# The expert stage of a streaming encoder layer, rebuilt in 33 blocks of 64 rows

## The chip, the cores and the metric

The kernel runs on one core of one Trainium2 chip. The metric is the device time of one execution in microseconds (us), lower is better. Engines: PE (TensorE, with its weight loads as PEld), DVE (VectorE), ACT (ScalarE), POOL (GpSimd) and SP (SyncE, which here only issues DMAs).

## The reference, cut to what matters

One layer of an encoder over 576 frames of width 1024: projections, a gated convolution, a gated delta rule, and then a mixture of experts with a residual and a final norm. The change is in the mixture, whose arithmetic is:

```python
for wg, wu, wd, c in experts:                # 32 experts, 1024 -> 256 -> 1024
    hdn = jax.nn.silu(t @ wg) * (t @ wu)
    acc = acc + c[:, None] * (hdn @ wd)      # c is zero but for 2 experts a frame
```

Each frame goes to two experts, so 1152 rows are spread over 32 experts. With the reference's inputs the fullest expert gets 75 rows, the next 61.

## The kernel before, in words

Phases 1 and 2 compute the mixers (up to about 937 us), phase 3 the norm, the router and the places of the rows, phase 4 the experts, phase 5 the weighted sum and the final norm.

At the end of phase 3 POOL scatters every row twice into the DRAM tensor `scr_rows`, sorted by expert (L1777). Phase 4 then takes one block of `BR = 80` rows for each expert. Were an expert fuller than 80 rows, the loop in `further_blocks` (L1364) would run more blocks; here none is needed.

Matrices are fp32, multiplied as sums of products of float32r numbers. ACT copies a tensor into a rounded high part (`ehi`, `xbh`, `hth`), DVE subtracts that from the tensor and writes the low part (`elo`, `xbl`, `htl`), and PE adds three products: high by high, low by high, high by low. A block goes through these steps:

- SP loads gate, up and down weights, 1 MB each, into `eraw` (L1615, L1619), and the rows into `xb` (L1676); two buffers of each.
- ACT splits the 4096 gate and up columns in one go (L1398) and the 2048 down columns in another (L1403); DVE follows with L1408.
- PE turns the rows with 8 transposes (`rows_turned`, L1318) into `wideA`; ACT and DVE split them (L1416, L1420).
- `gate_up` (L1321): 24 matmuls of 512 columns, whose stationary operand is 80 columns wide; gate in the left half of `proj[k]`, up in the right half, rows on the partitions.
- ACT takes the silu of gate (L1426), DVE multiplies by up (L1479), PE turns the result with 2 transposes (L1340), ACT and DVE split it (L1430, L1484).
- `down` (L1343): 12 matmuls into `wideB`; ACT copies that to `yout` (L1438), SP stores it to `scr_y` (L1680).

The order is written out by hand in `expert_tensor` (L1355), `expert_scalar` (L1440) and `expert_vector` (L1487). On PE a block's order is: 12 matmuls of `gate_up(b)`, `down(b-1)`, the other 12, the transposes of the rows of b+1, the transposes of the hidden layer of b. The next block's `gate_up` waits for `e_xl`, the low part of its rows, which were turned just before. Semaphores are counted up by each step; SP loads block b+2's weights once `e_low` says that block b's are split. SP's queue holds all loads and stores of the stage in one order.

After the last block POOL gathers each frame's two results with 10 indirect DMAs (L1791), and phase 5 adds and normalises.

Of the kernel before, what the change touches and what calls it, by code (L numbers as in the profile page):

```python
# [18 lines left out]
F32 = mybir.dt.float32  # L19
# [21 lines left out]
BR = 80  # L41
OVER = (SLOTS - 2) // BR
BLOCKS = EXPERTS + OVER
ROWS = SLOTS + BR

# [22 lines left out]
C_MISC = C_LEVEL + P * (LEVELS + 1)  # L68
# [23 lines left out]
def encoder_layer(nc, A, O):  # L92
# [6 lines left out]
    with top:  # L99
# [17 lines left out]
        before = const[:, C_BEFORE:C_BEFORE + P]  # L117

# [87 lines left out]
        EW = 24 * DE  # L206
        AT_P3 = EW

# [14 lines left out]

        p3 = area(AT_P3)
        g2row = sb(p3, "g2row", [P, D])
        wr = sb(p3, "wr", [P, KC, GROUPS + EXPERTS])
        tn = sb(p3, "tn", [P, UNITS, D])
        tT = [sb(p3, f"tT{k}", [P, D]) for k in range(2)]
        sqs = sb(p3, "sqs", [P, D])
        lg = sb(p3, "lg", [P, UNITS, GROUPS + EXPERTS])  # L230
# [8 lines left out]
        brow = sb(p3, "brow", [P, 3, OVER])  # L239

        eraw, ehi, elo = [None, None], [None, None], [None, None]
        ehi[0] = sb(p3, "ehi0", [P, EW], F32R)
        xb = [sb(p3, f"xb{k}", [P, D]) for k in range(2)]
        xbh = [sb(p3, f"xbh{k}", [P, KC, BR], F32R) for k in range(2)]
        xbl = [sb(p3, f"xbl{k}", [P, KC, BR], F32R) for k in range(2)]
        yout = [sb(p3, f"yout{k}", [P, D]) for k in range(2)]
        p3.close()
        p4 = area(0)
        eraw[0] = sb(p4, "eraw0", [P, EW])
        ehi[1] = sb(p4, "ehi1", [P, EW], F32R)  # L250
        elo[1] = sb(p4, "elo1", [P, EW], F32R)
        p4.close()
        p4 = area(AT_ML)
        elo[0] = sb(p4, "elo0", [P, EW], F32R)
        eraw[1] = sb(p4, "eraw1", [P, EW])
        hgate = [sb(p4, f"hgate{k}", [P, DE]) for k in range(2)]
        hid = [sb(p4, f"hid{k}", [P, DE]) for k in range(2)]
        hth = [sb(p4, f"hth{k}", [P, 2, BR], F32R) for k in range(2)]
        htl = [sb(p4, f"htl{k}", [P, 2, BR], F32R) for k in range(2)]
        p4.close()  # L260

        p5 = area(EW)
        fy = [[sb(p5, f"fy{j}_{c}", [P, D]) for c in range(UNITS)] for j in range(2)]
        fsq = sb(p5, "fsq", [P, D])
        p5.close()
        p5 = area(AT_ML + EW)
# [7 lines left out]
        x_in = [sem(f"x_in{c}") for c in range(UNITS)]  # L274
# [465 lines left out]
        def tails_pool(pool, i, which):  # L740
# [17 lines left out]
        p2_w, g_in = [sem("p2_w0"), sem("p2_w1")], [sem("gate_in0"), sem("gate_in1")]  # L758
# [8 lines left out]
        e_w, e_wd = [sem("e_w0"), sem("e_w1")], [sem("e_wd0"), sem("e_wd1")]  # L767
        e_x = [sem("e_x0"), sem("e_x1")]
        e_high, e_low, e_xt, e_xh, e_xl, e_gu, e_silu, e_hid, e_ht, e_hh, e_hl, e_dn, e_y = (
            sem("e_" + k) for k in "high low xt xh xl gu silu hid ht hh hl dn y".split())  # L770
# [3 lines left out]
        f_y = [sem(f"f_y{c}") for c in range(UNITS)]  # L774
# [242 lines left out]
        def out_split_high(act, q, k):  # L1017
            if isinstance(q, int):
                act.wait_ge(p2_w[k], 16 * (q // 2 + 1))
            else:  # L1020
                act.wait_ge(p2_w[k], 8 * (q - k) + 16)
# [114 lines left out]
        def phase3_scalar(act):  # L1136
# [15 lines left out]
            for part in range(2):  # L1152
                weights_high(act, 0, 0, part)
# [32 lines left out]
        def phase3_vector(dve):  # L1186
# [84 lines left out]
            link(dve.tensor_copy(table[0:1, TB_COUNT:TB_COUNT + 1], ex[0:1, 3, E - 1:E]))  # L1271
# [37 lines left out]
        DOWN_AT = 12  # L1309
        GU = 16 * DE  # L1310

        def rows_turned(pe, b, k, arrived=None):

            pe.wait_ge(*(arrived or (e_x[k], 8 * (b - k) + 16)))
            wait(pe, e_xl, b)
            v = xb[k][0:BR, :].rearrange("s (p c) -> s c p", c=KC)
            for c in range(KC):
                mm = pe.transpose(wideA[:, c * P:c * P + BR], v[:, c, :], ident[0:BR, 0:BR])  # L1318
            mm.then_inc(e_xt, 1)

        def gate_up(pe, b, k, between=None):  # L1321
            pe.wait_ge(e_low, 2 * b + 1)
            pe.wait_ge(e_xl, b + 1)
            wait(pe, e_hid, b - 1)
            for j in range(3 * KC):
                c, term = divmod(j, 3)
                if between and j == DOWN_AT:
                    between()
                x = (xbh, xbl, xbh)[term][k][:, c, :]
                w = (ehi, ehi, elo)[term][k][:, 0:GU].rearrange("p (w c n) -> p w c n", w=2, c=KC)[:, :, c, :]  # L1330
                mm = pe.matmul(proj[k][0:BR, :].rearrange("p (w n) -> p w n", w=2), x, w, start=(j == 0),  # L1331
                               stop=(j == 3 * KC - 1))
            mm.then_inc(e_gu, 1)

        def hidden_turned(pe, b, k):
            pe.wait_ge(e_hid, b + 1)
            wait(pe, e_hl, b)
            v = hid[k][0:BR, :].rearrange("s (p c) -> s c p", c=2)
            for c in range(2):
                mm = pe.transpose(proj[2][:, c * BR:(c + 1) * BR], v[:, c, :], ident[0:BR, 0:BR])  # L1340
            mm.then_inc(e_ht, 1)

        def down(pe, b, k):  # L1343
            pe.wait_ge(e_hl, b + 1)
            pe.wait_ge(e_low, 2 * b + 2)
            wait(pe, e_y, b)
            for n in range(2):
# [662 lines left out]
```

## Time and profile before

| | |
|---|---|
| runs of the kernel | 1411.27, 1421.46, 1423.44 us; median 1421.46 |
| the profiled execution | 1412.39 us |
| its span | 1410.7 us, so 1.7 us lie around it |
| granted PE clock over the span (1.00 is 2.4 GHz, 0.50 is 1.2 GHz) | 0.947 |
| busy share of the span | PE 88%, DVE 56%, ACT 44%, POOL 4% |
| first transpose of the expert stage | 989.85 us |
| last copy to `yout` begins | 1374.88 us |

A line of a timeline reads: start, duration (both us), engine, line, operation, output <- input with partitions x elements, and count; in brackets the idle time before it and what ended that. Matmuls overlap each other, so the time between two starts (the pitch) counts and not the duration.

### The profile page before, as it was taken

How to read it: one execution, taken by the hardware profiler on the slowest of the kernel's cores; microseconds unless marked ns; L12 is line 12 of the kernel's file. 1: busy time of each engine (PE TensorE's matmuls, PEld its weight loads, DVE VectorE, ACT ScalarE, POOL GpSimd, SP SyncE). 2: the span in 40 equal slices, each digit the busy share in tenths (PEclk: the TensorE clock that was granted, in tenths of full speed). 3: DMA queues.
4: the chain of work that ended last, by engine and by line, in shares of the span. 5: the costliest groups of instructions: out<-in, count | busy, mean ns of one | idle time of the engine just before them, and what ended most of it. 6: DMA issues, size and time to landing. Idle time of an engine off the chain costs nothing.

```text
span 1410.7 us, 22131 instructions
## 1 busy us (share of the span) xinstructions
PE 1247.0 (88%) x8469; PEld 1112.5 (79%) x8469; DVE 784.5 (56%) x930; ACT 622.3 (44%) x851; POOL 57.4 (4%) x124
## 2 busy tenths in 40 slices
PE   4989999999999999999989989980888888888870
PEld 4989999999999999999989989980555555555550
DVE  4437365473654736547465445236667667767735
ACT  4434343343433534335342322251566666666632
POOL 0000000000000000000000000004000000000002
PEclk9999999999999999999999999995799999999995
DMA  5271121111211111111202224543988888988836
GB/s 185 88 219 48 62 66 69 58 61 61 65 53 72 61 61 65 45 65 62 71 27 75 85 84 139 205 192 134 323 313 327 327 318 323 330 317 326 328 106 220
DMA packets 49434, 212.80 MB, mean 151 GB/s; under 512 B 5920, under 2 KB 8496, under 8 KB 37104
## 3 DMA queue, kind: packets, MB, share of 16 engines
q1 hardware_dynamic: 41200, 194.05, 39.2%
q0 software_dynamic: 2928, 10.05, 2.1%
q10 hardware_dynamic: 5264, 8.13, 1.6%
q8 instruction: 28, 0.46, 0.1%
q14 instruction: 14, 0.11, 0.0%
HBM read 181.25 MB, written 30.96 MB: 150 GB/s over the span
## 4 chain that ended last, share of the span: by engine, by line
PE 75%; DVE 10%; ACT 6%; issue 4%; DMA 3%; POOL 1%; SPq 0%; ACTq 0%; DVEq 0%; POOLq 0%
PE proj L614 22%; PE proj L1331 15%; PE wideB L1352 7%; PE proj L981 5%; PE wideA L377 4%; PE proj L924 3%; PE wideB L369 3%; PE wideB L383 2%; PE wideA L1318 2%; DVE xbl L1420 2%; PE small L981 2%; ACT xbh L1416 2%; DMA wraw<-in_w_in 1%; POOL scr_rows L1777 1%; DVE wlo L626 1%
## 5 line engine op out<-in xcount | busy, mean ns | idle before, releaser
L614 PE MATMUL proj<-xnh,whi 128*128 128x288 f32 x1152 | 349.2, 303 | 11.9 <-DVE xnl L1862 7.2
L614 PE MATMUL proj<-xnl,whi 128*128 128x288 f32 x1152 | 347.2, 301 | 0.0
L614 PE MATMUL proj<-xnh,wlo 128*128 128x288 f32 x1152 | 346.7, 301 | 0.0
L614 PEld LDWEIGHTS proj<-xnh,whi 128*128 128x128 f32 x1152 | 217.9, 189 | 13.1 <-issue 6.5
L1408 DVE TENSOR_TENSOR elo<-eraw,ehi 128x4096 fp32r<-128x4096 f32 x64 | 214.6, 3354 | 19.7 <-ACT ehi L1398 19.7
L614 PEld LDWEIGHTS proj<-xnl,whi 128*128 128x128 f32 x1152 | 217.9, 189 | 0.0
L614 PEld LDWEIGHTS proj<-xnh,wlo 128*128 128x128 f32 x1152 | 217.6, 189 | 0.0
L1331 PE MATMUL proj<-ehi,xbh 128*80 128x512 f32 x256 | 111.4, 435 | 34.0 <-DVE xbl L1420 34.0
L626 DVE TENSOR_TENSOR wlo<-wraw,whi 128x1024 fp32r<-128x1024 f32 x72 | 87.9, 1220 | 53.9 <-ACT whi L622 53.7
L1398 ACT ACTIVATE ehi<-eraw 128x4096 fp32r<-128x4096 f32 x32 | 116.1, 3628 | 0.4
L1331 PE MATMUL proj<-elo,xbh 128*80 128x512 f32 x256 | 109.7, 429 | 0.0
L1331 PE MATMUL proj<-ehi,xbl 128*80 128x512 f32 x256 | 109.6, 428 | 0.0
L622 ACT ACTIVATE whi<-wraw 128x1024 fp32r<-128x1024 f32 x72 | 76.1, 1057 | 57.5 <-PE proj L614 35.8
L1331 PEld LDWEIGHTS proj<-ehi,xbh 128*80 128x80 f32 x256 | 41.2, 161 | 59.8 <-issue 28.2
L1438 ACT ACTIVATE yout<-wideB 80x1024 f32<-80x1024 f32 x32 | 32.7, 1023 | 121.0 <-PE wideB L1352 121.0
L532 DVE TENSOR_TENSOR buf<-wideB,const 128x640 f32<-128x640 f32 (+1 forms) x48 | 38.5, 802 | 81.6 <-PE wideB L369 81.4
L453 ACT ACTIVATE TT<-wideB 128x640 f32<-128x640 f32 (+1 forms) x48 | 33.0, 687 | 87.6 <-PE wideB L383 87.6
L536 DVE TENSOR_TENSOR T<-T,wideA 128x640 f32<-128x640 f32 (+1 forms) x48 | 38.4, 799 | 59.7 <-PE wideA L377 59.7
L377 PE MATMUL wideA<-buf,TT 128*128 128x128 f32 x464 | 63.7, 284 | 3.4 <-DVE buf L532 3.4
L377 PEld LDWEIGHTS wideA<-buf,TT 128*128 128x128 f32 x464 | 55.5, 191 | 8.0 <-DVE buf L532 5.0
L1331 PEld LDWEIGHTS proj<-elo,xbh 128*80 128x80 f32 x256 | 41.8, 163 | 24.8 <-issue 6.7
L1479 DVE TENSOR_TENSOR hid<-proj,hgate 80x256 f32<-80x256 f32 x32 | 13.5, 421 | 85.4 <-ACT hgate L1426 85.4
(326 smaller groups left out, 2330.9 us busy)
## 6 DMA issues: line engine op xcount, KB each, us to landing
wraw<-in_w_in SPq DMA_DIRECT2D x72, 512.0 KB, 3.3
eraw<-in_w_gate SPq DMA_DIRECT2D x32, 1024.0 KB, 4.9
eraw<-in_w_up SPq DMA_DIRECT2D x32, 1024.0 KB, 7.3
eraw<-in_w_down SPq DMA_DIRECT2D x32, 1024.0 KB, 5.6
wraw<-in_w_out SPq DMA_DIRECT2D x24, 512.0 KB, 4.0
xb<-scr_rows SPq DMA_DIRECT2D x32, 320.0 KB, 6.1
scr_y<-yout SPq DMA_DIRECT2D x32, 320.0 KB, 5.8
scr_gate<-gate ACTq DMA_DIRECT2D x16, 288.0 KB, 2.1
```

Of the source, the lines that this page charges most:

```text
L369: mm = pe.matmul(wideB[:, U[u]], buf3[:, UW + u * P:UW + (u + 1) * P], T[:, U[u]], start=True, stop=True)
L377: mm = pe.matmul(wideA[:, U[u]], TT[:, U[u]], buf2[:, UW + u * P:UW + (u + 1) * P], start=True, stop=True)
L532: dve.tensor_tensor(units(buf2[:, UW:UW + w]), units(wideB[:, 0:w]), level_mask(k + 1, level_units(k)), ALU.mult).then_inc(s["x_set"], 1)
L614: mm = pe.matmul(out, w[:, kc, :], x[:, kc, hh * HALF:(hh + 1) * HALF], start=(j == 0), stop=(j == 23))
L622: act.activation(whi[t % 3][:, :, :], wraw[t % 3][:, :, :], ACT.Copy).then_inc(w_high, 1)
L626: dve.tensor_tensor(wlo[t % 3][:, :, :], wraw[t % 3][:, :, :], whi[t % 3][:, :, :].bitcast(F32), ALU.subtract).then_inc(w_low, 1)
L924: mm = pe.matmul(proj[h % 3][:, 0:HALF], w[:, kc, :], x[:, kc, hh * HALF:(hh + 1) * HALF], start=(j == 0), stop=(j == 23))
L981: mm = pe.matmul(banks[k][hh][:, 0:HALF], w[:, kc, :], x[:, kc, hh * HALF:(hh + 1) * HALF], start=(j == 0), stop=(j == 3 * KC - 1))
L1331: mm = pe.matmul(proj[k][0:BR, :].rearrange("p (w n) -> p w n", w=2), x, w, start=(j == 0), stop=(j == 3 * KC - 1))
L1352: mm = pe.matmul(wideB[0:BR, 512 * n:512 * (n + 1)], x, w, start=(j == 0), stop=(j == 5))
L1398: act.activation(ehi[k][:, 0:GU], eraw[k][:, 0:GU], ACT.Copy).then_inc(e_high, 1)
L1408: dve.tensor_tensor(elo[k][:, cols], eraw[k][:, cols], ehi[k][:, cols].bitcast(F32), ALU.subtract)\
```

## The change

A block now has 64 rows (`BR`), and there are always 33 of them (`NB`): one for each expert and one more for the first expert that has over 64 rows. Weights come into a ring of 5 places (`RING`); the low part is written over the raw one. The high and the low part of the rows stand side by side as one stationary operand of 128 columns (`xs`), so `gate_up` is 16 matmuls: all 8 with `ehi`, then all 8 with `elo`. Partitions 0 to 63 of the result belong to the high rows and 64 to 127 to the low ones; ACT copies the whole to `ysum` (`sums_copied`), and 4 fp32 matmuls with a constant of 128x64 (`fold`, two identities one above the other) add the halves and turn them at once. The 2 transposes of the hidden layer go. The row transposes, the fold, and `down` stand inside the next block's `gate_up`, and between blocks PE runs two fp32 products of constants, 128x512 each, whose result nobody reads (`held_warm`). Rows are loaded and results stored from POOL's queue; SP's holds the weights alone. The loops over blocks are written out.

```diff
-BR = 80
+BR = 64
+NB = EXPERTS + 1
+RING = 5
...
+        FOLD_AT, TURN_AT, DOWN_AT = 4, 6, 12
...
+        def gate_up(pe, b, r):
+            k = b % 2
             pe.wait_ge(e_xl, b + 1)
-            wait(pe, e_hid, b - 1)
-            for j in range(3 * KC):
-                c, term = divmod(j, 3)
-                if between and j == DOWN_AT:
-                    between()
...
+            wait(pe, e_sum, b - 1)
+            for j in range(2 * KC):
+                term, c = divmod(j, KC)
+                if j == FOLD_AT and b > 0:
+                    folded(pe, b - 1)
+                if j == TURN_AT and b < NB - 1:
+                    rows_turned(pe, b + 1)
+                if j == DOWN_AT and b > 0:
+                    down(pe, b - 1, (b - 1) % RING)
+                if c % HALF_KC == 0:
+                    pe.wait_ge((e_high, e_low)[term], 2 * b + 1 + c // HALF_KC)
+                w = (ehi[k], elo[r])[term][:, :].rearrange("p (w c n) -> p w c n", w=2, c=KC)[:, :, c, :]
+                mm = pe.matmul(proj[k][:, :].rearrange("p (w n) -> p w n", w=2), xs[k][:, c, :], w, start=(j == 0),
+                               stop=(j == 2 * KC - 1))
             mm.then_inc(e_gu, 1)
...
+        def held_warm(pe):
+
+            for j in range(2):
+                pe.matmul(small[:, :], ident, const[:, P:P + 512], start=True, stop=True)
+
+        def folded(pe, b):
+
+            pe.wait_ge(e_sum, b + 1)
+            wait(pe, e_hid, b)
+            for j in range(4):
+                mm = pe.matmul(proj[2][:, j * BR:(j + 1) * BR], ysum[b % 2][:, j * P:(j + 1) * P], fold,
+                               start=True, stop=True)
+            mm.then_inc(e_fold, 1)
...
         def phase4_tensor(pe):
...
+            rows_turned(pe, 0)
+            for b in range(NB):
+                gate_up(pe, b, b % RING)
+                if b < NB - 1:
+                    held_warm(pe)
+            folded(pe, NB - 1)
+            down(pe, NB - 1, (NB - 1) % RING)
...
+        def weights_high(act, b, r, half):
+            act.wait_ge(e_w[r], 32 * (b // RING) + 32)
+            wait(act, e_gu, b - 1)
+            act.activation(weights_half(ehi[b % 2], half), weights_half(eraw[r], half), ACT.Copy).then_inc(e_high, 1)
+
+        def down_high(act, b, r):
+            act.wait_ge(e_wd[r], X_DONE + 16 * (b // RING) + 16)
+            wait(act, e_dn, b)
+            act.activation(dhi[:, :], draw[r][:, :], ACT.Copy).then_inc(d_high, 1)
...
+        def sums_copied(act, b, k):
             act.wait_ge(e_gu, b + 1)
-            wait(act, e_hid, b - 1)
-            act.activation(hgate[k][0:BR, :], proj[k][0:BR, 0:DE], ACT.Silu).then_inc(e_silu, 1)
+            wait(act, e_fold, b - 1)
+            act.activation(ysum[k][:, :], proj[k][:, :], ACT.Copy).then_inc(e_sum, 1)
...
         def phase4_scalar(act):
             rows_high(act, 0, 0)
...
+            for b in range(NB):
+                if b > 0:
+                    sums_copied(act, b - 1, (b - 1) % 2)
+                if b < NB - 1:
+                    weights_high(act, b + 1, (b + 1) % RING, 0)
+                if b > 0:
+                    silu_gate(act, b - 1)
+                if b < NB - 1:
+                    rows_high(act, b + 1, (b + 1) % 2)
+                if b > 0:
+                    hidden_high(act, b - 1, (b - 1) % 2)
+                if b < NB - 1:
+                    weights_high(act, b + 1, (b + 1) % RING, 1)
+                if b > 0:
+                    y_copy(act, b - 1, (b - 1) % 2)
+                down_high(act, b, b % RING)
...
         def phase4_vector(dve):
             rows_low(dve, 0, 0)
...
+            for b in range(NB):
+                if b > 0:
+                    down_low(dve, b - 1, (b - 1) % RING)
+                    hidden_set(dve, b - 1)
+                    hidden_low(dve, b - 1, (b - 1) % 2)
+                if b < NB - 1:
+                    rows_low(dve, b + 1, (b + 1) % 2)
+                    weights_low(dve, b + 1, (b + 1) % RING, 0)
+                    weights_low(dve, b + 1, (b + 1) % RING, 1)
...
-            for k in range(2):
-                gate_up_load(k, k, e_w[k])
-                down_load(k, k, e_wd[k])
+            for r in range(RING - 1):
+                gate_up_load(r, r, e_w[r])
+                down_load(r, r, e_wd[r])
...
             sp.wait_ge(spread_rows, 16 * 2 * UNITS)
+            gate_up_load(RING - 1, RING - 1, e_w[RING - 1])
+            down_load(RING - 1, RING - 1, e_wd[RING - 1])
+            for b in range(RING, NB):
+                r = b % RING
...
+                sp.wait_ge(e_gu, b - RING + 1)
+                gate_up_load(e, r, e_w[r])
+                sp.wait_ge(e_dn, b - RING + 1)
+                down_load(e, r, e_wd[r])
...
             pool.wait_ge(spread_rows, 16 * 2 * UNITS)
+            pool.wait_ge(nx["out"], 16)
...
+            for b in range(2):
+                rows_load(b, b)
+            for b in range(2, NB):
+                if b == EXPERTS:
+                    pool.wait_ge(route, ROUTE_STEPS)
+                pool.wait_ge(e_xt, b - 1)
+                rows_load(b, b % 2)
+                if b > 2:
+                    y_store(b - 3, (b - 3) % 2)
+            for b in range(NB - 3, NB):
+                y_store(b, b % 2)
```

Besides, the down weights are read so that a partition gets two pieces of 4 KB in place of one of 8 KB, and `fx`, the residual for phase 5, is loaded once block 29 is through instead of after the last split.

## Rows read from the trace of the kernel before

**Rows 1.** Chain of waits, 1140 to 1180 us: start, us, what.
```profile
1154.76 0.86 PE wideA L1318 x8
...
1155.64 0.71 ACT xbh L1416
...
1156.38 0.83 DVE xbl L1420
...
1157.33 3.00 PE proj L1331 x12
1160.33 2.75 PE wideB L1352 x12
1163.08 2.78 PE proj L1331 x12
...
1168.36 4.37 PE proj L1331 x12
```
**Rows 2.** Timeline: the row transposes of block 1 and of block 31.
```profile
1001.29 1.01 PE L1318 MATMUL wideA<-const,xb 80*128 80x80 f32 x8
...
1353.64 1.01 PE L1318 MATMUL wideA<-const,xb 80*128 80x80 f32 x8
```
**Rows 3.** Stretches: length, busy us (count) of PE, PEld, DVE, ACT, POOL, clock, DMA share, GB/s.
```profile
830.00:850.00 20.00, 20.00 (x153) 20.00 (x152) 10.69 (x15) 4.91 (x6) 0.00 (x0) 1.00 0.37 124
...
990.00:1020.00 30.00, 25.64 (x103) 16.81 (x103) 19.14 (x12) 18.39 (x13) 0.00 (x0) 0.79 0.91 326
...
1140.00:1180.00 40.00, 36.15 (x158) 23.93 (x156) 25.71 (x17) 26.32 (x23) 0.00 (x0) 0.91 0.87 324
```
**Rows 4.** Timeline of one block, 1160 to 1190 us: ACT and DVE.
```profile
1163.20 1.02 ACT L1438 ACTIVATE yout<-wideB 80x1024 f32<-80x1024 f32 x1 [2.99 <-PE wideB L1352]
...
1164.12 1.90 ACT L1403 ACTIVATE ehi<-eraw 128x2048 fp32r<-128x2048 f32 x1
...
1167.46 0.30 ACT L1430 ACTIVATE hth<-proj 128x160 fp32r<-128x160 f32 x1
...
1168.22 2.28 DVE L1408 TENSOR_TENSOR elo<-eraw,ehi 128x2048 fp32r<-128x2048 f32 x1
...
1170.42 0.32 DVE L1484 TENSOR_TENSOR htl<-proj,hth 128x160 fp32r<-128x160 f32 x1
```
**Rows 5.** Timeline: fp32 matmuls, two instructions each, 128 and 36 columns.
```profile
749.65 1.28 PE L346 MATMUL wideB<-kT 128*128 128x128 f32 x10
...
945.66 1.87 PE L1172 MATMUL small<-wr,tT 128*128 128x36 f32 x16
```
**Rows 6.** Timeline: the stage's first loads and matmuls, the last copy, the first gather.
```profile
986.50 1.48 SPq L1676 DMA_DIRECT2D xb<-scr_rows  x2
...
989.85 1.33 PE L1318 MATMUL wideA<-const,xb 80*128 80x80 f32 x8 [28.61 <-DMA xb<-scr_rows]
...
993.00 0.69 PE L1331 MATMUL proj<-ehi,xbh 128*80 128x512 f32 x1 [1.81 <-DVE xbl L1420]
...
1374.88 1.02 ACT L1438 ACTIVATE yout<-wideB 80x1024 f32<-80x1024 f32 x1 [3.45 <-PE wideB L1352]
...
1379.77 0.99 POOL L1791 DMA_INDIRECT fy<-scr_y,slot_y  x1 [397.72 <-DMA scr_y<-yout]
```
**Rows 7.** DMA: a stretch with weight loads alone, then queue and issues, 990 to 1350 us.
```profile
918.00:920.00 2.00, 1.00 1.02 426
...
q1 hardware_dynamic: 18671, 113.85, 86.9%
...
xb<-scr_rows SPq DMA_DIRECT2D x30, 320.0 KB, 6.1
```
**Rows 8.** Timeline: POOL's scatter beside DVE's splits.
```profile
964.02 6.63 DVE L1408 TENSOR_TENSOR elo<-eraw,ehi 128x4096 fp32r<-128x4096 f32 x2
964.06 5.29 POOL L1777 DMA_INDIRECT scr_rows<-tn,slot_row  x1 [83.38 <-DVE block_table L1263]
...
971.80 0.95 POOL L1777 DMA_INDIRECT scr_rows<-tn,slot_row  x1 [0.30 <-issue]
```

More of the change, by code:

```diff
@@ L117, in encoder_layer @@
         before = const[:, C_BEFORE:C_BEFORE + P]
+        fold = const[:, C_FOLD:C_FOLD + BR]
         def level_mask(k, count=UNITS):
@@ L260, in encoder_layer @@
-        p4.close()
-        p5 = area(EW)
+        p3.close()
+        p3 = area(AT_WR)
+        wr = sb(p3, "wr", [P, KC, GROUPS + EXPERTS])
+        p3.close()
+        AT_YBL, AT_LATE = AT_YB, AT_MIX + 6 * D // 4
+        gu_at = [0, GU, AT_YBL, AT_LATE + DN, AT_TN]
+        dn_at = [2 * GU, AT_LATE, AT_LATE + DN + GU, AT_LATE + 2 * DN + GU, AT_TN + GU]
+        eraw, elo, draw, dlo = [], [], [], []
+        for r in range(RING):
+            for place, plain, low, width, name in ((gu_at[r], eraw, elo, GU, "gu"), (dn_at[r], draw, dlo, DN, "dn")):
+                p4 = area(place)
+                plain.append(sb(p4, f"{name}_raw{r}", [P, width]))
+                p4.close()
+                p4 = area(place)
+                low.append(sb(p4, f"{name}_lo{r}", [P, width], F32R))
+                p4.close()
@@ new lines, in encoder_layer @@
+        p4 = area(AT_GD)
+        ehi = [None, sb(p4, "ehi1", [P, GU], F32R)]
+        xb = [None, sb(p4, "xb1", [P, D])]
+        ehi[0] = sb(p4, "ehi0", [P, GU], F32R)
+        dhi = sb(p4, "dhi", [P, DN], F32R)
+        p4.close()
+        p4 = area(AT_TN + GU + DN)
+        xs = [sb(p4, f"xs{k}", [P, KC, 2 * BR], F32R) for k in range(2)]
+        yout = [sb(p4, f"yout{k}", [P, D]) for k in range(2)]
+        ysum = [sb(p4, f"ysum{k}", [P, 2 * DE]) for k in range(2)]
+        p4.close()
+        p4 = area(AT_YB - D)
@@ L263, in encoder_layer @@
+        xb[0] = sb(p4, "xb0", [P, D])
+        p4.close()
+        p4 = area(AT_YBL + GU)
+        hs = [sb(p4, f"hs{k}", [P, 2, 2 * BR], F32R) for k in range(2)]
+        p4.close()
+        p4 = area(AT_LATE + 3 * DN + GU)
+        hgate = sb(p4, "hgate", [P, 2, BR])
+        hid = sb(p4, "hid", [P, 2, BR])
+        p4.close()
+        p5 = area(0)
         fy = [[sb(p5, f"fy{j}_{c}", [P, D]) for c in range(UNITS)] for j in range(2)]
+        p5.close()
+        p5 = area(AT_YBL)
         fsq = sb(p5, "fsq", [P, D])
@@ L273, in encoder_layer @@
         par_in = sem("par_in")
-        x_in = [sem(f"x_in{c}") for c in range(UNITS)]
+        e_wd = [sem(f"x_or_down_in{r}") for r in range(RING)]
+        X_DONE = 16
         zeroed = sem("zeroed")
@@ L766, in encoder_layer @@
         spread_rows = sem("spread_rows")
-        e_w, e_wd = [sem("e_w0"), sem("e_w1")], [sem("e_wd0"), sem("e_wd1")]
+        e_w = [sem(f"e_w{r}") for r in range(RING)]
+        f_y = [sem(f"f_y{c}") for c in range(UNITS)]
         e_x = [sem("e_x0"), sem("e_x1")]
-        e_high, e_low, e_xt, e_xh, e_xl, e_gu, e_silu, e_hid, e_ht, e_hh, e_hl, e_dn, e_y = (
-            sem("e_" + k) for k in "high low xt xh xl gu silu hid ht hh hl dn y".split())
+        e_high, e_low, d_high, d_low, e_xt, e_xh, e_xl, e_gu, e_sum, e_fold, e_silu, e_hid, e_hh, e_hl, e_dn, e_y = (
+            sem("e_" + k) for k in "high low dhigh dlow xt xh xl gu sum fold silu hid hh hl dn y".split())
         e_out = [sem("e_out0"), sem("e_out1")]
@@ L1151, in phase3_scalar @@
                     act.activation(tT[c % 2][:, :], wide(c)[:, :], ACT.Copy).then_inc(nx["copied"], 1)
-            for part in range(2):
-                weights_high(act, 0, 0, part)
+            weights_high(act, 0, 0, 0)
+            weights_high(act, 0, 0, 1)
             act.wait_ge(route, R_GAP)
@@ L1372, in further_blocks @@
             return count
+        FURTHER = 3
         def phase4_tensor(pe):
[L1375 to L1390 removed]
@@ L1452, in phase4_scalar, with hidden_low @@
+        def hidden_low(dve, b, k):
+            dve.wait_ge(e_hh, b + 1)
+            dve.tensor_tensor(hs[k][:, :, BR:2 * BR], hid[:, :, :], hs[k][:, :, 0:BR].bitcast(F32), ALU.subtract)\
+               .then_inc(e_hl, 1)
         def phase4_scalar(act):
             rows_high(act, 0, 0)
-            expert_scalar(act, 0, 0, first=True)
-            for b in range(1, 4):
-                expert_scalar(act, b, b % 2)
-            with act.Fori(2, EXPERTS // 2 - 1) as i:
-                for k in range(2):
-                    expert_scalar(act, 2 * i + k, k)
```

363 lines of the change are left out of this document (164 added, 199 removed).

## The prediction

> **What bounds the kernel now.** I read the page first (where the chain of waits spends its time, and the clock), then the chain over some blocks of the expert stage, the timeline of one block, the stretches with clock and DMA share, the DMA view, and the two ends of the stage. The chain of one block [rows 1] runs over PE, ACT, DVE and back to PE: 3.00 + 2.75 + 2.78 us for 36 matmuls (a pitch of 2.75 / 12 = 0.229 us), 0.86 for the row transposes, and then PE stands still while ACT (0.71) and DVE (0.83) split the rows that were just turned. With hand-overs that is 1168.36 - 1157.33 = 11.03 us, of which PE lacks work for some 1.7. The mean period is longer, (1353.64 - 1001.29) / 30 = 11.75 us [rows 2], because the clock falls now and then: the next 12 matmuls took 4.37 us in place of 3.00, and the stretch had a granted clock of 0.91; the stage opens at 0.79, while a stretch in which PE was busy throughout had 1.00 [rows 3]. So PE with its pause and its clock sets the end; the loads do not, though DMA is busy 87 to 91% of the time.
>
> **The change part by part: PE's own work.** A block keeps 12 matmuls of down and needs 16 for 24 in gate and up: 28 x 0.229 = 6.41 us, 1.83 less. Transposes stay at 0.86. The fold is 4 fp32 products, 8 instructions; with 36 columns such an instruction took 1.87 / 16 = 0.117 us at most [rows 5], and I take 0.11 for 64 columns: 0.89. The fp32 products of constants have 512 columns: an instruction with 128 took between 0.11 and 0.128 us (1.28 for 10, end included), so one with 512 some 0.44 to 0.51, and four of them 1.8 to 2.0. The sum is 6.41 + 0.86 + 0.89 + 1.8 = 10.0 us a block. By itself that is no gain over the 9.1 us of matmuls and row transposes before, and a 33rd block comes on top. The gain must come from the pause and the clock.
>
> **ACT's chain through a block.** ACT does everything in one order, so I follow the new loop. Durations [rows 4]: a copy out of PSUM costs 0.30 us for 160 elements and 1.02 for 1024, so 0.59 for 512 and 0.27 for 128; a split of 2048 columns costs 1.90 on ACT and 2.28 on DVE; DVE's small operations 0.29 (from 0.32 for 160). A hand-over from PE costs 0.12 (1163.08 to 1163.20 [rows 1, 4]), others 0.05 to 0.08, ACT operations in a row overlap by 0.1, and a matmul group begun after a wait costs 0.25 more than one that runs on (3.00 against 2.75).
> From the end of down(b-1): copy of y to 1.14; split of down(b) to 2.95; copy of the sums to 3.45; PE starts the fold at 3.53 and ends it at 4.66. PE meanwhile ran 4 matmuls (0.92), the products of constants (1.8) and 4 matmuls (0.92), 3.6 us together: the products stand almost exactly in the wait for the sums, so I cost them at nothing. Without that cover they would be worth 1.8 us a block. Then 2 matmuls to 5.12, row transposes to 5.98, ACT's high rows to 6.69, the high hidden layer to 6.87, DVE's low one to 7.21, and down(b) starts at 7.29, about when PE's 6 matmuls are through (7.35). It ends at 10.29. The rows split here are those of the next block, so that wait is gone; what is late next is this loop of copy, split, copy, fold, silu and split. For the changes between fp32 and fp32r matmuls, which I price between 0 and the 0.25 of a start each, I take 0.1 twice. Period: 10.5 us (10.0, where PE alone counts, to 10.9).
> ACT is busy 0.59 + 3 x 1.90 + 0.27 + 0.59 + 0.27 + 1.02 = 8.4 us of it, DVE 3 x 2.28 + 0.69 + 2 x 0.29 = 8.1; both fit. DVE's first split, of down(b-1), queues ahead of the hidden product; it can run from 2.95 to 5.3, before the silu is there.
>
> **Loads.** A block's weights are 3.15 MB; alone they ran at 426 GB/s [rows 7], 7.4 us. The queue was busy 86.9% of 360 us = 313 us for 30 blocks, 10.4 us a block; less 7.4 that leaves 3.0 for 80 rows in and out, and 2.4 to 3.0 for 64. So 9.8 to 10.4 us a block against a period of 10.5, with four blocks loaded before the stage starts: hidden. Weights now wait only for PE's last use of a ring place; behind SP's waits stand only other weights.
> Row loads and stores go to POOL's queue. The load of rows b+1 is queued behind the store of y(b-3), which is ready 0.2 us after gate_up(b-2); it has until the transposes 4.2 us after gate_up(b-1), thus 10.5 + 4.0 = 14.5 us. Two issues at 0.95 + 0.30 [rows 8] and a landing of 6.1 [rows 7] need 8.6, which leaves 5.9 to spare.
>
> **The ends.** The first rows were issued at 986.50, turned at 989.85, and multiplied from 993.00 [rows 6]. POOL issues them now, beside 3 MB of weights; I add 2 us (0 to 2.8, the landing of 6.1 [rows 7] against the 3.3 from issue to first use): 995. Block 0 runs its 16 matmuls and 8 transposes partly at the lower clock: 4.5 us at the full one, twice that at half, I take 7: 1002. 32 periods later it is 1338. Then, by the same steps, sums at +2.5, fold +3.7, hidden layer +5.1, down +8.2, copy +9.35: 1347.4, against 1374.88 + 1.02 = 1375.9 before. From there to the first gather took 3.9 us, and I add 1 for a store by POOL (0 to 4.3 [rows 8]). The rest, 1410.7 - 1379.77 = 30.9, stays. Span 1383.2, execution 1384.9, against 1412.39. The median of the runs lay 9.07 above the profiled execution; two of four executions were at that upper level, so I add half: 1389.
>
> **The Trainium skill.** POOL stood 5.29 us at its first scatter while DVE ran two splits, and 0.95 later [rows 8]: 4.34 more, about one split of 4096 columns. The page "SBUF — State Buffer", section "Who interferes with whom", says that descriptors of a DMA issued from GpSimd's queue are written through a port that certain DVE operations lock for a whole instruction, and advises the SP or ACT queue; this change goes the other way. [...] It is the fourth rival below.
>
> **Rivals.** *PE alone sets the period*, the hand-overs all being covered: 10.0, 32 x 0.5 = 16 us less, 1373. For it: the loop and PE are close. Against: three hand-overs lie in the loop.
> *The clock falls as before* [rows 3]: at a mean of 0.94, PE's two thirds of the loop stretch by 6%, 0.45 us a block, 1403; if all stretched, 1411. Against: the pause of 1.7 us that stands ahead of the falls is filled.
> *Loads bind.* If weights came at no more than the 326 GB/s of the mixed stretch [rows 3], 3.67 MB a block would take 11.3 us; 28 blocks from about 1000 end at 1316, just where block 31's split wants them; with rows at 3.0 us on top it is some 13 us late, 1402. Against: 426 GB/s.
> *POOL's row loads come late*, the slower side. Each POOL DMA can lose a DVE split, now 2.28 us. One for each of the two a block is 4.6 and inside the 5.9 to spare; three are 6.8, and the period becomes 11.4, 1419; four are 9.1, and it is 8.6 + 9.1 - 4.0 = 13.7, 32 x 3.2 = 102 us more, 1491. It decides from 5.9 us of loss a block. For it: [rows 8]. Against: DVE pauses some 2 us a block.
>
> **How the numbers follow.** Forecast 0.60 (1376 to 1402 by itself), PE alone 0.10, clock 0.12, loads 0.10, late rows 0.08. Faster by over 1% (under some 1407; 1% is about what a measurement of this kernel can tell from no change): 0.60 + 0.10 + 0.10 + half the clock's = 0.86; within 1%: 0.06; slower: 0.08. The range runs from 1364, PE alone with the profiled level of the runs, to 1412, the clock's worst.
>
> **What would show it.** Right: 33 blocks at 10.3 to 10.7 us, no wait of PE for the split rows, clock 0.98 or more after block 0, fold waiting under 0.3 us for the sums. Wrong: row transposes waiting for `xb`, ACT's splits waiting for weights, matmul pitches of 0.43 within the stage, PE's idle time put down to "issue".

## The result and the profile after

The kernel after takes 1395.71 us (median of 4 runs, 1394.57 to 1397.89) against 1416.82 for the kernel before beside it (4 runs, 1411.27 to 1423.44): a ratio of 0.9856, interval 0.9818 to 0.9894. A second comparison with more runs gave 1396.46 against 1413.04, 0.987 (0.9839 to 0.9901). The profiled execution took 1395.9 us, its span 1394.2, at a mean clock of 0.949. The kernel before has two groups of times, 10 us apart (experiment 2), and its median depends on how many runs fall in each. By these medians the kernel is faster by 1.3 to 1.4%. The forecast was 1389, in a range of 1364 to 1412: the sign and the range are right, the time lies 6.7 us above the forecast.

The expert stage itself did what was forecast. This is the chain of waits over one block of the kernel after (start, us, what), to set beside [rows 1]:

```profile
1150.19 0.93 PE proj L1365 x4
1151.11 1.72 PE small L1372 x4
1152.83 0.92 PE proj L1365 x4
1153.76 0.93 PE proj L1379 x8
1154.68 0.52 PE proj L1365 x2
1155.21 1.03 PE wideA L1347 x8
1156.23 1.57 PE proj L1365 x6
1157.81 2.76 PE wideB L1393 x12
```

There is no ACT, no DVE and no "issue" in it: every piece is PE's, end to start. The steps ACT 0.71 and DVE 0.83, in which PE stood still for the split of the rows, are gone. The sum of the eight pieces is one period, 10.38 us; the row transposes of block 1 and of block 32 in the timeline of the kernel after give the mean, (1331.64 - 1010.00) / 31 = 10.38 us, where [rows 2] had 11.75:

```profile
1010.00 1.15 PE L1347 MATMUL wideA<-const,xb 64*128 64x64 f32 x8
...
1331.64 1.09 PE L1347 MATMUL wideA<-const,xb 64*128 64x64 f32 x8
```

ACT's operations cost what was taken from [rows 4]; here they are for one block of the kernel after (timeline):

```profile
1151.15 1.90 ACT L1464 ACTIVATE dhi<-dn_raw 128x2048 fp32r<-128x2048 f32 x1
1152.94 0.58 ACT L1493 ACTIVATE ysum<-proj 128x512 f32<-128x512 f32 x1
```

The copy of the sums ends at 1153.52 and PE is through with its four matmuls at 1153.75, so the fold starts without a wait.

Where the other part of the time went is seen ahead of the stage. The timeline of the kernel before, then of the kernel after, at the places that [rows 6] show for before:

```profile
933.73 0.38 SPq L1671 DMA_DIRECT2D scr_x<-x  x1
...
936.94 1.46 PE L1167 MATMUL wideA<-const,tn 128*128 128x128 f32 x8 [4.10 <-DVE tn L1193]
...
951.97 0.35 DVE L1220 TENSOR_TENSOR lg<-small,const 128x180 f32<-128x180 f32 x1 [7.36 <-PE small L1172]
```

```profile
935.62 0.38 SPq L1757 DMA_DIRECT2D scr_x<-x  x1
...
938.83 1.94 PE L1195 MATMUL wideA<-const,tn 128*128 128x128 f32 x8 [4.10 <-DVE tn L1221]
...
964.22 0.35 DVE L1248 TENSOR_TENSOR lg<-small,const 128x180 f32<-128x180 f32 x1 [17.24 <-PE small L1200]
...
995.22 0.34 SPq L1701 DMA_DIRECT2D gu_raw<-in_w_gate  x1
...
996.71 0.58 POOL L1858 DMA_DIRECT2D xb<-scr_rows  x1 [4.35 <-issue]
...
1004.52 1.14 PE L1347 MATMUL wideA<-const,xb 64*128 64x64 f32 x8 [31.02 <-DMA xb<-scr_rows]
...
1007.15 2.93 PE L1365 MATMUL proj<-ehi,xs 128*128 128x512 f32 x6 [1.48 <-DVE xs L1487]
...
1352.35 1.11 PE L1393 MATMUL wideB<-dhi,hs 128*64 128x512 f32 x2 [1.61 <-DVE hs L1517]
...
1357.77 1.02 ACT L1508 ACTIVATE yout<-wideB 64x1024 f32<-64x1024 f32 x1 [5.80 <-PE wideB L1393]
...
1363.12 1.00 POOL L1883 DMA_INDIRECT fy<-scr_y,slot_y  x1 [3.50 <-DVE stats L1603]
```

From the first matmul of the stage to the end of its last copy it is 1358.79 - 1007.15 = 351.6 us, and 382.9 before: 31.3 us gained. But the stage starts at 1007.15 and not at 993.00. Of these 14.2 us, 1.9 lie ahead of the router stage (the store of the residual, `scr_x<-x`, is issued at 935.62 against 933.73; over all traces of kernels with the change it lies between 934.23 and 936.92, so this part is spread), 10.4 in the router stage (from that store to the reading of the logits 28.6 us, before 18.2), 4.5 in the landing of the first rows (7.81 us from issue to transposes, before 3.35), and 2.5 are won back (the placing of the rows 2.0, the first split 0.5). What lies behind the stage grew by 0.6. The sum, 14.2 - 31.3 + 0.6 = -16.5, is the whole difference of the spans.

The 10.4 us are clock. Stretches of the kernel before, then of the kernel after (columns as in [rows 3]):

```profile
938.00:940.00 2.00, 2.00 (x10) 1.76 (x9) 1.55 (x3) 1.57 (x2) 0.00 (x0) 0.50 1.03 410
...
942.00:944.00 2.00, 2.00 (x21) 2.00 (x20) 1.17 (x3) 1.81 (x4) 0.00 (x0) 1.00 0.00 0
```

```profile
942.00:944.00 2.00, 2.00 (x12) 2.00 (x11) 0.74 (x2) 1.97 (x4) 0.00 (x0) 0.50 1.04 416
...
950.00:960.00 10.00, 10.00 (x50) 10.00 (x49) 0.00 (x0) 3.47 (x3) 0.00 (x0) 0.50 0.01 3
...
1004.00:1014.00 10.00, 8.00 (x29) 6.08 (x30) 2.88 (x3) 5.21 (x5) 1.02 (x2) 0.50 0.47 138
...
1140.00:1180.00 40.00, 40.00 (x187) 27.23 (x186) 29.98 (x24) 31.28 (x32) 4.24 (x8) 1.00 1.01 362
```

In both kernels PE stands 4.10 us ahead of the router stage's first transposes (those at 936.94 before, at 938.83 after), and the clock falls to 0.50. In the profile of before it was back at 1.00 by 942; in that of after it stayed at 0.50 to the end of the stage although PE was busy for 10.00 of 10.00 us, and it was still there when block 0 began. From 1018 on it is 1.00, up to the last block.

### The profile page after: what moved, and what is told of

Read it like the earlier page. It is cut to its first block, busy times and chain, and to the rows that moved or that the text cites. A ratio compares the mean times of both kernels' runs of the same rounds, so it can differ in the third digit from the quotient of the medians.

```text
span 1394.2 us, 21931 instructions
## 1 busy us (share of the span) xinstructions
PE 1264.6 (91%) x8577; PEld 1135.5 (81%) x8577; DVE 785.5 (56%) x969; ACT 637.3 (46%) x923; POOL 90.7 (7%) x190
## 4 chain that ended last, share of the span: by engine, by line
PE 79%; DVE 7%; ACT 5%; DMA 4%; issue 3%; POOL 1%; SPq 0%; ACTq 0%; DVEq 0%; POOLq 0%
PE proj L641 24%; PE proj L1365 10%; PE wideB L1393 7%; PE proj L1009 5%; PE wideA L404 4%; PE small L1372 4%; PE proj L952 3%; PE wideB L396 3%; PE wideA L1347 2%; PE proj L1379 2%; PE wideB L410 2%; PE small L1009 2%; DMA wraw<-in_w_in 2%; PE small L1200 1%; POOL scr_rows L1848 1%
## 5 line engine op out<-in xcount | busy, mean ns | idle before, releaser
L1468 DVE TENSOR_TENSOR gu_lo<-gu_raw,ehi 128x2048 fp32r<-128x2048 f32 x66 | 147.9, 2283 | 0.0
L1459 ACT ACTIVATE ehi<-gu_raw 128x2048 fp32r<-128x2048 f32 x66 | 125.7, 1906 | 0.0
L1365 PE MATMUL proj<-ehi,xs 128*128 128x512 f32 x264 | 97.7, 473 | 1.5 <-DVE xs L1487 1.5
L1473 DVE TENSOR_TENSOR dn_lo<-dn_raw,dhi 128x2048 fp32r<-128x2048 f32 x33 | 75.7, 2293 | 39.2 <-ACT dhi L1464 39.2
L1393 PE MATMUL wideB<-dhi,hs 128*64 128x512 f32 x264 | 84.0, 400 | 1.6 <-DVE hs L1517 1.6
L1365 PE MATMUL proj<-gu_lo,xs 128*128 128x512 f32 x264 | 72.8, 399 | 0.0
L1347 PEld LDWEIGHTS wideA<-const,xb 64*128 64x128 f32 x264 | 31.6, 199 | 43.4 <-DMA xb<-scr_rows 31.4
L1347 PE MATMUL wideA<-const,xb 64*128 64x64 f32 x264 | 36.2, 280 | 31.0 <-DMA xb<-scr_rows 31.0
L1365 PEld LDWEIGHTS proj<-ehi,xs 128*128 128x128 f32 x264 | 45.8, 193 | 22.5 <-issue 15.3
L1464 ACT ACTIVATE dhi<-dn_raw 128x2048 fp32r<-128x2048 f32 x33 | 62.6, 1896 | 0.0
## 6 DMA issues: line engine op xcount, KB each, us to landing
gu_raw<-in_w_up SPq DMA_DIRECT2D x33, 1024.0 KB, 12.2
```

The source lines that it names most:

```text
L1347: mm = pe.transpose(wideA[:, c * BR:(c + 1) * BR], v[:, c, :], ident[0:BR, 0:BR])
L1365: mm = pe.matmul(proj[k][:, :].rearrange("p (w n) -> p w n", w=2), xs[k][:, c, :], w, start=(j == 0), stop=(j == 2 * KC - 1))
L1393: mm = pe.matmul(wideB[0:BR, 512 * n:512 * (n + 1)], x, w, start=(j == 0), stop=(j == 5))
L1459: act.activation(weights_half(ehi[b % 2], half), weights_half(eraw[r], half), ACT.Copy).then_inc(e_high, 1)
L1464: act.activation(dhi[:, :], draw[r][:, :], ACT.Copy).then_inc(d_high, 1)
L1468: dve.tensor_tensor(weights_half(elo[r], half), weights_half(eraw[r], half), weights_half(ehi[b % 2], half).bitcast(F32), ALU.subtract).th ...
```

## The experiments

**1. Keep PE busy through the pause ahead of the router stage.** Theory A: the 10 us are lost to the clock there. Rival B: the transposes and logits are slow beside the loads, whatever PE did before.

```diff
         def phase3_tensor(pe):
+            for j in range(4):
+                pe.matmul(proj[2][:, :], ident, const[:, P:P + 512], start=True, stop=True)
             pe.wait_ge(p3_in, 32)
```

> The changed kernel with four fp32 products of constants at the head of the router stage, where PE stood 4.1 us before the first transposes. Theory A (the stage gained what was forecast, some 31 us; 10 us were lost ahead of it because PE's clock fell in that pause and stayed at 0.50): the router stage runs at 1.00, logits are through 10 us earlier, 1385 us. Rival B (the router stage was late for another reason, the 12 MB of weights loaded beside it for instance): no change, 1394 to 1398, and if the products only stand in the way, up to 3 us more.

Measured: 1381.54 us (1380.8 to 1383.57), 0.9741 (0.968 to 0.9802) of before. The timeline shows the four products in the pause and the router's transposes at the full clock; the logits are read at 953.51:

```profile
935.44 3.60 PE L1189 MATMUL proj<-const 128*128 128x512 f32 x8
939.70 1.06 PE L1197 MATMUL wideA<-const,tn 128*128 128x128 f32 x8 [0.66 <-DVE tn L1223]
```

The same 8 transposes take 1.94 us in the kernel after. Theory A holds: with the pause filled the time is 1395.71 - 1381.54 = 14.2 us lower by the medians. By the two traces the span is 12.3 us shorter, of which the router stage gives 11.6 (17.0 us from the store to the logits for 28.6).

**2. The same products in the kernel before.**

The edit is that of experiment 1, in the same place.

> The kernel before with the same four products at the head of the router stage. Theory A (the fall of the clock there is a chance that both kernels have, and makes the two levels of the runs before, 1411 to 1412 and 1421 to 1423): all runs at the lower level, 1409 to 1413, within 3 us of each other, so the changed kernel with the products is then some 26 us faster than this one. Rival B (the change brought the fall): nothing changes here, the two levels stay.

Measured: 1411.81 us, all ten runs between 1410.51 and 1413.66. The kernel before beside it had two groups of times, 9 runs at 1410.8 to 1414.0 and 10 at 1422.3 to 1425.2; over all comparisons of the study, the first ones aside, 19 of 37 runs lie below 1416 and 18 above 1419. With the products the upper group is gone. Over those 37 runs the mean granted clock is 0.945 to 0.947 in the lower group and 0.938 to 0.940 in the upper one. So the two groups of the kernel before, 10 us apart, are this clock (no run of the upper group has a trace; the clocks of the runs and this experiment say it), and with the clock held in both kernels the change is worth 1411.81 - 1381.54 = 30.3 us: the 31 of the stage.

**3. Leave out the products of constants between blocks.** The calls of `held_warm` go (an output that nobody reads). Theory A: they cost nothing, and nothing hangs on them. Rival C: they hold the clock. Rival D: they cost their 1.72 us a block.

```diff
                 gate_up(pe, b, b % RING)
-                if b < NB - 1:
-                    held_warm(pe)
```

> The changed kernel without the two products of constants between blocks. Theory A (they stand in PE's wait for the copy of the sums, and cost nothing): period 10.2 to 10.4 us as before, 1392 to 1397. Rival C (they hold the clock): PE waits 1.7 us a block, the clock falls to a mean of about 0.94 as in the kernel before, period 10.9 or more, 1412 or more. Rival D (PE's work alone sets the period): period 10.39 - 1.72 = 8.7, 1341.

Measured: 1411.9 us (1398.63 to 1419.41, 10 runs), 0.9933 (0.9889 to 0.9978) of before. Chain of waits, a stretch of 100 us and PE's waits over the stage, all of this kernel:

```profile
1169.40 0.02 issue
...
1170.46 1.69 issue
1172.15 0.58 ACT ysum L1491
1172.73 0.04 issue
1172.78 1.11 PE proj L1379 x8
```

```profile
1200.00:1300.00 100.00, 85.97 (x402) 60.84 (x401) 71.95 (x56) 71.18 (x73) 9.55 (x18) 0.93 0.96 334
```

```profile
PE proj L1379 <- ACT ysum L1491: 48.4, 31, 1.6
```

The chain now goes through ACT. Without the products PE stands 1.6 us in every block for the sums (48.4 us in 31 waits), and a block at the full clock lasts 10.39 us as before (one `down` ends at 1169.40, the next at 1179.79): the products stand in a wait and cost nothing. But the clock drops to 0.93, matmuls run at half speed now and then, and the mean period is 10.85. That is rival C. From its first matmul to its last copy the stage takes 369.2 us for 351.6, 17.6 more: 0.47 us in each of 31 periods are 14.6, and 2.9 lie behind the last row transposes. That is over half of the 31.3 that the stage had gained. The medians differ by less, 1411.9 - 1396.46 = 15.4 us, because three of the ten runs here, 1398.63 to 1400.04 at a mean clock of 0.944 to 0.945, lie 10 us and more below the other seven (clock 0.928 to 0.937, the profiled one among them). That looks like the two groups of the kernel before; none of the three has a trace.

**4. Let the first rows go ahead of the fifth ring place's weights.**

```diff
             sp.wait_ge(spread_rows, 16 * 2 * UNITS)
+            for k in range(2):
+                sp.wait_ge(e_x[k], 16)
             gate_up_load(RING - 1, RING - 1, e_w[RING - 1])
```

> The changed kernel, but SP loads the fifth ring place only when the rows of blocks 0 and 1 have landed. Theory A (first transposes came 7.8 us after the row load was issued, against 3.4 before, because 3 MB of weights went ahead of it): 3.5 to 4.5 us between them, some 4 us less, 1391 to 1392. Rival E (a load issued by POOL is slow by itself): still 7 to 8 us, 1395 or a little more.

Measured: 1388.66 us (1387.63 to 1392.99), 0.9804 (0.974 to 0.9867). In the timeline the rows now take 998.81 - 995.34 = 3.47 us to the transposes, not 7.81:

```profile
995.34 0.58 POOL L1860 DMA_DIRECT2D xb<-scr_rows  x1 [4.38 <-issue]
...
998.81 1.15 PE L1347 MATMUL wideA<-const,xb 64*128 64x64 f32 x8 [26.69 <-DMA xb<-scr_rows]
```

So the 3 MB issued just ahead delayed them by 4.3 us. The time fell by 1395.71 - 1388.66 = 7.1 us, the span of the profiled execution by 8.3: 4.3 here, 1.4 ahead of the rows' issue (the spread of that part), and 2.7 between the first matmul and the last copy (349.0 for 351.6), where the clock came back by 1006, 4.6 us after the first matmul, and not after some 10 us. That the earlier rows bring this about is not shown: in experiment 9's trace it was back some 4 us after the first matmul, at 1002, with a landing of 7.78 us.

**5. The kernel after once more, with more runs.**

> The changed kernel once more, for its levels. Theory A (the clock's fall at the head of the router stage is a matter of chance for both kernels): besides runs at 1394 to 1398 there are some near 1384 to 1387, ten less, as the kernel before had 12 of 23 at its lower level. Rival B (the change makes the fall certain): all at 1394 to 1398.

Measured: 1396.46 us, six runs between 1393.95 and 1397.14. With the first four that makes ten of ten in one group, where the kernel before had two (of the 23 runs that the expectation counts, 11 were at the lower level and not 12). It does not make the late return of the clock certain for this code: see experiments 3 and 6.

**6. Four products between blocks in place of two.** Theory: PE sets the period, and what is added shows. Rival: there is slack beside them.

```diff
         def held_warm(pe):
...
-            for j in range(2):
+            for j in range(4):
```

> The changed kernel with four products of constants between blocks for two. Theory A (PE's work and the loop over ACT are level at 10.4 us, so whatever is added to PE shows in full): period 10.39 + 1.72 = 12.1 us, 32 x 1.72 = 55 us more, 1450. Rival G (something else sets 10.39, the loads at a DMA share of 1.00 for instance): less than 1.72 a block, 1400 to 1430.

Measured, one run: 1435.82. The chain of waits:

```profile
1155.21 1.59 PE proj L1365 x6
...
1160.47 3.44 PE small L1372 x8
...
1167.21 1.59 PE proj L1365 x6
```

The period is 12.00, 1.62 more for two more products of 1.72: what is added shows. The stage takes 402.4 us, 50.7 more. The time is below the expected one because in this run the router stage had its clock back in time (logits read at 953.89), at a DMA share of 1.01 from the same loads. Up to there this kernel is the kernel after:

```profile
942.00:944.00 2.00, 2.00 (x19) 2.00 (x18) 0.74 (x2) 1.97 (x5) 0.00 (x0) 0.89 1.01 406
```

**7. Half a megabyte more weights in each block from the sixth**, into a place nobody reads, to find whether the loads are near their limit: the DMA share of the stage was 1.01.

```diff
+            sp.wait_ge(route, ROUTE_STEPS)
             for b in range(RING, NB):
...
                 gate_up_load(e, r, e_w[r])
+                wait(sp, more, 16 * (b - RING))
+                sp.dma_start(again[:, :], A["w_gate"][at(e), :, :].rearrange("a (p c) n -> (a p) (c n)", p=P)[:, 0:1024])\
+                  .then_inc(more, 16)
```

> The changed kernel with 0.5 MB more of weights loaded for each block from the sixth on, into a place that nobody reads. Theory A (the loads have room, the share of 1.00 only says that the ring always has something to load): period still 10.4 us, about 400 GB/s, 1394 to 1398. Rival H (at 355 GB/s beside rows in and out the DMA is at its limit): still about 355 GB/s, so 11.8 us a block; the lead of the ring takes some 25 us of the 28 x 1.4 = 39, weights come late in the last blocks, 1405 to 1420.

Measured, one run: 1394.84. PE is still busy throughout, at the same pitch, with more bytes a second. The kernel after, then this one:

```profile
1100.00:1300.00 200.00, 200.00 (x928) 136.14 (x927) 151.31 (x116) 152.08 (x155) 20.84 (x40) 1.00 1.00 355
```

```profile
1100.00:1300.00 200.00, 200.00 (x931) 136.40 (x930) 152.15 (x116) 151.74 (x155) 20.30 (x39) 1.00 1.02 389
```

The mean period is (1330.62 - 1008.95) / 31 = 10.38 as before. The loads had room: at a DMA share of 1.0 the bytes still rose by a tenth. How much more there is, is not shown. SP, which here waits for the extra load of the block before, issued the extra loads every 10.9 us in the mean (1039.43 to 1311.71 for 25 blocks) and not every 10.38, and the last down weights went out at 1312.14, for 1305.96 in the kernel after. So the loads fell behind PE, and the lead of the ring kept that from showing in 33 blocks.

**8. Row transposes five matmuls later.**

```diff
-        FOLD_AT, TURN_AT, DOWN_AT = 4, 6, 12
+        FOLD_AT, TURN_AT, DOWN_AT = 4, 11, 12
```

> The changed kernel, with the row transposes of the next block behind 11 of the 16 matmuls of gate and up instead of behind 6, so that ACT's high rows and the small steps behind them come later. Theory A: the loop over ACT has no slack, since it stands level with PE at 10.39 us; PE then waits for the hidden layer ahead of down, about 1.1 us a block, the period is 11.4 to 11.5, and the time about 1431. Theory B: the loop has a slack of about a microsecond under PE's own work: a period of 10.4 to 10.7 and 1396 to 1406.

Measured, one run: 1426.22, about 30 us more. PE waits 0.78 us ahead of every `down`, and the period is 1159.73 - 1148.35 = 11.38 (timeline):

```profile
1148.35 0.67 PE L1393 MATMUL wideB<-dhi,hs 128*64 128x512 f32 x2 [0.78 <-DVE hs L1517]
...
1159.73 0.67 PE L1393 MATMUL wideB<-dhi,hs 128*64 128x512 f32 x2 [0.78 <-DVE hs L1517]
```

Five matmuls at a pitch of 0.23 are 1.15 us, and the period grew by 1.00. So the path from the row transposes over ACT and DVE to `down` had little slack, an estimated 0.15 us. It is one part of the loop over ACT. For the other, over the copy of the sums, experiment 3 gives 10.39 beside PE's own 10.38: PE and the loop are level.

**9. Load ring places 2 and 3 only after the logits.** Is it the 12 MB of weights beside the router stage that hold the clock down?

```diff
-            for r in range(RING - 1):
+            for r in range(2):
...
+            sp.wait_ge(nx["logits"], UNITS)
+            for r in range(2, RING - 1):
+                gate_up_load(r, r, e_w[r])
+                down_load(r, r, e_wd[r])
```

> The changed kernel, with the weights of ring places 2 and 3 loaded only once the router's last logits are through (before: ahead of the router stage, beside its transposes). Theory A: the loads that run beside the first transposes of the router stage keep PE's clock at half after its pause of 4.1 us. Without them the clock comes back by 944 to 946 us in most executions, logits are read at 953 to 955 us, and the median is 10 us lower, 1385 to 1388. Theory B: the loads have nothing to do with it. Then the profiled execution shows a clock of 0.50 to the end of the stage, logits at 963 to 966, and a median of 1394 to 1398 as before, or two levels of times 10 us apart.

Measured: 1394.93 us, one run at 1383.04 and four at 1394.85 to 1396.47. The one at 1383.04 is the profiled one, and there the clock came back at 943:

```profile
942.00:944.00 2.00, 2.00 (x14) 2.00 (x12) 0.28 (x2) 1.97 (x5) 0.00 (x0) 0.60 0.65 256
944.00:946.00 2.00, 2.00 (x21) 2.00 (x21) 1.21 (x2) 1.93 (x5) 0.00 (x0) 1.00 0.00 0
```

Theory A wanted most of the runs there, and one of five is not most. Together with the run of experiment 6, where it came back in spite of the loads, this speaks against the loads of places 2 and 3 as the cause. Those of places 0 and 1 still ran beside the first transposes (a DMA share of 1.03 in 940 to 942), and no run is without them.

**10. A better version.** First the parts of experiments 1 and 4 together, with 24 products ahead of block 0 and the two also behind the last block:

```diff
+            for j in range(12):
+                held_warm(pe)
             rows_turned(pe, 0)
             for b in range(NB):
                 gate_up(pe, b, b % RING)
-                if b < NB - 1:
-                    held_warm(pe)
+                held_warm(pe)
```

> The changed kernel with the four products at the head of the router stage, with the fifth ring place loaded after the first rows, with 24 products of constants before the first row transposes, and with two more after the last block. Each gain by its own step: 14 us from the router stage (as measured alone), 4.3 from the rows' landing (as measured alone), some 2.9 because block 0 runs at the full clock (8.4 us of matmuls and transposes against 5.5), 2.4 because the last down does. Theory A (they add up): 1395.7 - 23.6 = 1372, no pitch of 0.43 us after the router stage. Rival F (the 24 products run at the lower clock, 1.7 us each, and are late): first transposes wait for PE, 1380 to 1390.

Measured: 1378.15 us (1375.63 to 1379.75), 0.9736 (0.9695 to 0.9777). It is 6 us short of what was expected. In the profiled execution the products ran out 4.5 us before the rows came, and block 0 began at half clock; experiment 11 asks whether that is the reason (timeline):

```profile
989.94 1.14 PE L1349 MATMUL wideA<-const,xb 64*128 64x64 f32 x8 [4.54 <-DMA xb<-scr_rows]
992.56 2.93 PE L1367 MATMUL proj<-ehi,xs 128*128 128x512 f32 x6 [1.48 <-DVE xs L1490]
```

**11. The same with 28 products ahead of block 0, and one between the last fold and the last `down`.**

```diff
-            for j in range(12):
+            for j in range(14):
                 held_warm(pe)
...
             folded(pe, NB - 1)
+            pe.matmul(small[:, :], ident, const[:, P:P + 512], start=True, stop=True)
             down(pe, NB - 1, (NB - 1) % RING)
```

> The six-part version (products of constants in PE's pause ahead of the router stage, rows loaded ahead of the fifth ring place, products between the placing of the rows and block 0), with 28 instead of 24 products ahead of block 0 and one more product between the last fold and the last down. Theory A: PE's remaining waits of 4.54 and 1.61 us are what let the clock fall, so block 0's half-clock part (2.9 us) and the slow end of the last down (1 to 1.5 us) come back: 1373.5 to 1375 against 1378.15. Theory B: the clock falls whatever stands there, or the products delay as much as they save: 1377 to 1380.

Measured: 1376.88 us (1374.14 to 1377.36), 0.9706 (0.9659 to 0.9753); the profiled run is the one at 1374.14.

```profile
989.29 1.10 PE L1349 MATMUL wideA<-const,xb 64*128 64x64 f32 x8 [0.77 <-DMA xb<-scr_rows]
991.87 1.65 PE L1367 MATMUL proj<-ehi,xs 128*128 128x512 f32 x6 [1.48 <-DVE xs L1491]
```

With a wait of 0.77 in place of 4.54 the first six matmuls take 1.65 us and not 2.93, and the last `down` 3.01 from its start to the copy (1333.28 to 1336.29) and not 4.39: theory A by the profile. By the time it is only 1.3 us under experiment 10, between the two expectations; the runs of the two overlap, so that much is not shown, and the missing 6 us of experiment 10 stay unexplained by the time. It has the lowest time of the study, 19 us under the kernel after.

## Why the prediction was right, and where it missed

*The forecast of the stage* held, in part because two errors cancel (below): first matmul to last copy 352.4 forecast, 351.6 measured, and 30.3 us of gain with the clock held on both sides (experiments 1 and 2).

*The period.* Forecast 10.5 from ACT's loop, measured 10.38. Its parts moved against each other. PE's own work was put at 10.0: 28 matmuls at 6.41, transposes 0.86, fold 0.89, products 1.8. Measured are 6.70, 1.03, 0.93 and 1.72, together 10.38. The matmuls were too cheap because 0.229 is the pitch within a run of 12, and each change of work between them adds some: the 2 behind the fold took 0.52 and the 6 behind the row transposes 1.57, a pitch of 0.26. ACT's loop, put at 10.29 and 0.2, came out at 10.39 without the products (experiment 3). So the bound is PE and the loop at once, where I had the loop alone; the rival "PE alone", 1373, fell with PE's own work of 10.0.

*The products of constants cost nothing.* Right as a cost (experiment 3: a period of 10.39 either way), but their worth was only hinted at by the rival on the clock: without them PE stands 1.6 us in each block for the sums, the clock drops, and the stage loses 17.6 us. The forecast's argument that "the pause of 1.7 us that stands ahead of the falls is filled" carries over half of the gain.

*Loads hidden.* Right, with some room that the DMA share of 1.0 does not show: 389 GB/s in experiment 7 against 355.

*POOL's queue.* Right: in the stage its issues took 0.53 us, not 0.95, also beside DVE's splits, and no block waited for its rows. The Trainium skill, "SBUF — State Buffer", section "Who interferes with whom", named beside the fourth rival, puts a stall of descriptors down to other DVE operations than these: a split is a `TENSOR_TENSOR` with two inputs, and by that section such a one contends with a GpSimd instruction that reads SBUF and not with one that only writes it. The direct loads and stores of the stage, 0.53 us beside such splits, agree with that, and so does the first scatter, which reads its places from `slot_row`. It stood 3.16 us for 0.95 of a later one, and it ended 0.9 us after the first of the two splits (timeline of the kernel after; a split of 2048 columns takes 2.29):

```profile
976.27 4.50 DVE L1468 TENSOR_TENSOR gu_lo<-gu_raw,ehi 128x2048 fp32r<-128x2048 f32 x2
976.32 3.16 POOL L1848 DMA_INDIRECT scr_rows<-tn,slot_row  x1 [93.50 <-DVE block_table L1291]
```

The first scatter of [rows 8] too ended 0.9 us after the first split there, of 4096 columns and 4.43 us. That the read is what POOL waited with was not tried.

*Block 0 and the end.* Block 0 and 32 periods were put at 343 us and took 1347.17 - 1007.15 = 340.0. From there to the end of the last copy I had 9.4 us, and it took 11.6: PE waits 2.47 for the sums and 1.61 for the hidden layer, with no products to fill them, and the last `down` runs at half clock, 5.4 us for 3.0. The first error took 3.0 us off and the second put 2.3 on.

*The step that failed* is "the first rows ... I add 2 us: 995". The stage began at 1007.15. Of the 12.2 us too few, 2.5 are the landing: 4.5 where I took 2 and bounded it by 2.8, because behind 3 MB of weights issued just ahead the rows took 7.81 us to their first use, more than the 6.1 of [rows 7] that I had as the worst, and 3.47 without these weights ahead (experiment 4). Nearly all the rest is the router stage, which I took over from the profiled execution at its own clock. That execution was one of the kernel before's lower group, and I allowed for the upper group with half of 9.07 us. I had seen the two groups as a spread of the runs; they are two ways through one stage, and the kernel after took the slower one ten times in ten. That the time still came within 6.7 us is luck in part: the 4.5 us of the upper group were added as a mean of two groups, and stood in for a loss of 10.4. With the clock up, the sum against the profiled execution comes out near: 1384.9 forecast, 1383.04 in the one run of experiment 9 that had it. There, too, two errors cancel: the stage began 2.6 us late and was 4.5 shorter.

What stays open is why the clock stays down in most executions of the new code and in about half (18 of 37) of the old. It is no certainty: seven traces have the same code and the same loads up to the end of the router stage (the kernel after and experiments 3, 4, 5, 6, 7 and 8), and in one of them, experiment 6, the clock came back; three runs of experiment 3 look like it. The loads beside the stage were the first suspect; experiments 6 and 9 speak against those of places 2 and 3. Whether it is the moment at which PE's pause falls was not tried.

*What would show it:* periods of 10.3 to 10.7, no wait for the split rows, a clock of 1.00 after block 0, and the fold without a wait are all there. Of the signs for "wrong", pitches of 0.43 show in block 0 (8 matmuls from 1012.10 to 1015.51) and in the last `down`, none between; row transposes wait for `xb` in block 0 alone. Most of what was lost lay ahead of the stage, where I had set no sign.

## What to carry to other kernels

Read the runs' spread as a question: here two groups of times 10 us apart were two ways through one stage, and the stretches with their clock told which stage it was. Where PE pauses for a few microseconds ahead of a stage of small products, try filling the pause: four products of constants there were worth 14 us in the kernel after, nearly half as much as the whole rebuilt stage. And when a wait inside a loop is filled with idle products, count what they protect: here they cost nothing and kept 17.6 us of the stage's 31.3.

## What was not expected of the hardware

The clock, once at 0.50, stayed there for some 25 us in the router stage while the profile shows PE busy without a gap (10.00 of 10.00 us in 950 to 960), with transposes and products of 36 columns; in the run of experiment 6 the same instructions had it back within some 5 us. The Trainium skill, "TensorE: Matmul & The Clock Gate", section "What's actually happening", has activity release the throttle; here PE's busy share does not tell whether it will.

Between 1100 and 1300 us, weights and rows together ran at 389 GB/s in experiment 7, where the kernel after had a DMA share of 1.00 at 355 GB/s. The share did not tell what was left.
